# A hybrid transformer pair on one core: the latent's key and value products moved into the shared weight stream

## The reference, cut to what matters

```python
c_kv = rms_norm(c_kv, kv_norm_w)                       # 512 tokens x 128
k_rope = partial_rope(k_rope, cos, sin)
q_rope = partial_rope(q[..., :ROPE_DIM], ...)
# keys of 8 heads:   c_kv @ w_uk   (128 -> 8 x 48, padded with zeros to 8 x 64)
# values of 8 heads: c_kv @ w_uv   (128 -> 8 x 64)
# an indexer keeps the 128 best keys of each query; softmax over them; values
```

## Time and profile before

| what | value |
|---|---|
| median of 3 runs | 2507.4 us (2507.02 to 2508.23) |
| the profiled execution, its own time | 2504.52 us |
| its span, first to last instruction | 2502.8 us |
| TensorE matmul busy | 98% of the span |
| GpSimd, VectorE, ScalarE busy | 51%, 42%, 42% |
| chain that ended last | PE 90%, DVE 7%, ACT 3% |
| granted clock | 0.996 of full speed |
| DMA queue q1, share of 16 engines | 26.1% |

### The profile page before, as it was taken

One profiled execution on the slowest core, in us unless ns is written; L12 is line 12 of the kernel. 1 busy time (PEld: TensorE's weight loads), 2 busy tenths in 40 slices (PEclk: granted clock), 3 DMA queues, 4 the chain that ended last, 5 costly groups with the idle time before them and its releaser, 6 DMA issues.

```text
span 2502.8 us, 32082 instructions
## 1 busy us (share of the span) xinstructions
PE 2459.2 (98%) x12462; PEld 2014.1 (80%) x12462; DVE 1052.6 (42%) x2017; ACT 1042.2 (42%) x1584; POOL 1282.8 (51%) x1774
## 2 busy tenths in 40 slices
PE   8999999999999999999999999999999999999998
PEld 6777888888777787888878888877977788888886
DVE  7966525322795552422342113198265433311101
ACT  5334666323524467532443233332356524322221
POOL 5544645555553464555555554584433355554543
PEclk9999999999999999999999999999999999999999
DMA  4332112222222212232322232332222122232322
GB/s 156 93 104 75 60 59 82 89 100 96 92 92 72 85 51 76 68 99 95 111 93 100 93 101 85 135 110 69 92 69 68 65 96 98 89 100 94 100 94 83
DMA packets 63090, 224.45 MB, mean 90 GB/s; under 512 B 7335, under 2 KB 8871, under 8 KB 62812
## 3 DMA queue, kind: packets, MB, share of 16 engines
q1 hardware_dynamic: 61308, 216.62, 26.1%
q0 software_dynamic: 1632, 5.78, 0.8%
HBM read 219.70 MB, written 3.99 MB: 89 GB/s over the span
## 4 chain that ended last, share of the span: by engine, by line
PE 90%; DVE 7%; ACT 3%; issue 0%; DMA 0%; SPq 0%; DVEq 0%; ACTq 0%
PE proj L186 77%; PE proj L874 1%; PE att L911 1%; PE att L186 1%; DVE hT L543 1%; PE att L853 1%; PE att L897 1%; PE att L969 1%; PE att L864 1%; PE att L955 1%; DVE h_low L537 1%; PE att L2095 1%; ACT b_logits L2457 1%; ACT probs L1111 0%; PE att L2070 0%
## 5 line engine op out<-in xcount | busy, mean ns | idle before, releaser
L163 POOL TENSOR_TENSOR weight_low<-ring,weight_high 128x256 fp32r<-128x256 f32 x1584 | 1216.8, 800 | 1067.8 <-ACT weight_high L133 1046.1
L186 PE MATMUL proj<-h_high,weight_high 128*128 128x512 f32 x2000 | 787.4, 394 | 3.8 <-DVE h_low L537 1.5
L186 PE MATMUL proj<-h_high,weight_low 128*128 128x512 f32 x2000 | 779.4, 390 | 0.0
L186 PE MATMUL proj<-h_low,weight_high 128*128 128x512 f32 x2000 | 779.2, 390 | 0.0
L133 ACT ACTIVATE weight_high<-ring 128x1024 fp32r<-128x1024 f32 x391 | 412.0, 1054 | 406.9 <-PE proj L186 375.6
L186 PEld LDWEIGHTS proj<-h_high,weight_high 128*128 128x128 f32 x2000 | 375.6, 188 | 98.6 <-ACT sq_ L1010 5.3
L186 PEld LDWEIGHTS proj<-h_low,weight_high 128*128 128x128 f32 x2000 | 375.6, 188 | 79.0
L186 PEld LDWEIGHTS proj<-h_high,weight_low 128*128 128x128 f32 x2000 | 375.9, 188 | 75.2
L2678 DVE TENSOR_TENSOR b_big<-proj,b_big 128x512 f32<-128x512 f32 x42 | 29.0, 691 | 376.3 <-PE proj L186 376.3
L186 PE MATMUL proj<-b_act_high,weight_high 128*128 128x512 f32 x352 | 137.4, 390 | 0.0
L186 PE MATMUL proj<-b_act_high,weight_low 128*128 128x512 f32 x352 | 137.1, 389 | 0.0
(11 more groups left out here) (481 smaller groups left out, 3606.1 us busy)
## 6 DMA issues: line engine op xcount, KB each, us to landing
ring<-in_stream SPq DMA_DIRECT2D x396, 512.0 KB, 3.3
xT<-in_x SPq DMA_DIRECT2D x4, 512.0 KB, 6.3
idx<-gate_rows POOLq DMA_DIRECT2D x8, 256.0 KB, 4.3
out<-hT SPq DMA_DIRECT2D x4, 512.0 KB, 2.7
bias_rows<-bias_row SPq DMA_DIRECT2D x2, 512.0 KB
b_logits<-in_mem POOLq DMA_DIRECT2D x1, 1024.0 KB, 5.6
bias_rows<-bias_row SPq DMA_DIRECT2D x1, 768.0 KB
consts<-in_const SPq DMA_DIRECT2D x1, 704.0 KB, 10.2
```

Source lines behind the costliest of these rows:

```text
L163: self.s_low.on(pool.tensor_tensor(self.low[:, c % self.slots, cols], self.raw[:, c % self.slots, cols], self.high[:, c % HIGH, cols], ALU ...
L186: mm = pe.matmul(out, a, b, start=(k == 0 and i == 0), stop=(k == n - 1 and i == 2))
```

## The change

The 128 x 128 pieces of the key weights and the 128 x 512 value weights become tiles of the weight stream, in the order in which they are used. Together they are one chunk per layer. The eight products per layer go through `Weights.product`: the latent is split into `ckv_high` (ScalarE, after the move of za1) and `ckv_low` (VectorE, after top-k round 6), and each plain matmul becomes three rounded ones. The two direct loads per layer disappear. The value groups are reordered: vv0 and vv1 follow sbk0, vv2 and vv3 follow sbk1, nothing follows sbk2 and sbk3. As one key piece of 128 columns lies between dense tiles, chunks no longer end where groups end: chunk 17 of the layer ends inside sbq1 (step 6 of 0 to 7), 18 in sbq2 (step 5), 19 in sbq3 (step 4), 20 in sbk0 (step 3), and chunk 21 holds the rest of sbk0 and all value weights, so its last user is vv3. From sbk1 on a dense tile is a whole chunk again.

```diff
 def layer_tiles():
-    t += [(f"{n}{i}", KD, P) for n in ("q", "za", "zb", "sbq", "sbk") for i in range(4)]
+    t += [(f"{n}{i}", KD, P) for n in ("q", "za", "zb") for i in range(4)]
+    for i in range(4):
+        t += [(f"sbq{i}", KD, P), (f"kk{i}", 1, P)]
+    t += [("sbk0", KD, P), ("vv", 1, T)] + [(f"sbk{i}", KD, P) for i in range(1, 4)]
...
+LATENT_VALUES = [(0, 1), (2, 3), (), ()]
...
-                pe.wait_ge(s_ckv.sem, s_ckv.base + 1)
-                pe.wait_ge(s_lat.sem, s_lat.base + 32)
-            G.close(pe.matmul(out[:, :], wuk[:, i * P:(i + 1) * P], ckv, start=True, stop=True))
-        for b in range(TB):
-            dense(f"sbk{b}")
-            out = G.open(pe, f"vv{b}")
-            G.close(pe.matmul(out[:, :], ckv[:, b * P:(b + 1) * P], wuv, start=True, stop=True))
+                pe.wait_ge(s_ckv_low.sem, s_ckv_low.base + 1)
+            W.product(pe, f"kk{i}", out[:, :], [(ckv_high, ckv_low)])
+        for i in range(4):
+            dense(f"sbk{i}")
+            for b in LATENT_VALUES[i]:
+                out = G.open(pe, f"vv{b}")
+                c = slice(b * P, (b + 1) * P)
+                W.product(pe, f"vv{b}", out[:, :], [(ckv_high[:, c], ckv_low[:, c])], tokens=True)
...
             move(f"za{i}", za[:, i, :], ACT.Silu)
+            if i == 1:
+                act.wait_ge(s_ckv.sem, s_ckv.base + 1)
+                s_ckv_high.on(act.activation(ckv_high, ckv, ACT.Copy))
...
-        for b in range(TB):
-            if b == 0 and l == 0:
+        for i in range(4):
+            if i == 0 and l == 0:
                 act.wait_ge(S.s_rows.sem, 16)
-            move(f"sbk{b}", sk[:, b, :])
-            if b == 0:
+            move(f"sbk{i}", sk[:, i, :])
+            if i == 0:
                 act.wait_ge(s_rq.sem, s_rq.base + 4)
-            move(f"vv{b}", dv[:, b, :])
+            for b in LATENT_VALUES[i]:
+                move(f"vv{b}", dv[:, b, :])
...
+        def latent_low():
+
+            dve.wait_ge(s_ckv_high.sem, s_ckv_high.base + 1)
+            s_ckv_low.on(dve.tensor_tensor(ckv_low, ckv, ckv_high, ALU.subtract))
...
+            if i == 6:
+                latent_low()
...
-        s_lat.on(sp.dma_start(wuk, A["wuk"][l]), 16)
-        s_lat.on(sp.dma_start(wuv, A["wuv"][l]), 16)
```

More of the change, by code:

```diff
@@ L228, in layer_tile_of @@
             of[f"{n}{i}"] = f"{n}_half{i // TB}"
+    for b in range(TB):
+        of[f"vv{b}"] = "vv"
     return of
@@ L255, in layer_groups @@
     for i in range(4):
-        g += [(f"sbk{i}", "a"), (f"vv{i}", "a")]
+        g += [(f"sbk{i}", "a")] + [(f"vv{b}", "a") for b in LATENT_VALUES[i]]
     for p in range(PAIRS_H):
@@ L622, in hybrid_layers @@
     onehot, table, toep = flat_v[:, 0:ROW], flat_v[0:33, ROW:ROW + 12], flat_k[0:12, 0:ROW]
+    ckv_high, ckv_low = (rounded(n, [P, T], mix_at + 4 * (CAUSAL + i * T))[:, :] for n, i in (("ckv_high", 2), ("ckv_low", 3)))
     mlo, zc = sq_, sk
@@ L649, in hybrid_layers @@
     key_turn = tflat[KEY:KEY + 32, 3 * T:4 * T]
-    s_lat = sem("s_lat", 32)
+    s_ckv_high = sem("s_ckv_high", 1)
+    s_ckv_low = sem("s_ckv_low", 1)
     s_signs = sem("s_signs", 1)
@@ L1645, in keys @@
             s_keys.on(sp.dma_start(dk[64 * hh:64 * hh + ROPE, :, :], src), 16)
-    return {"keys": keys, "lead": lead_of(DEPTH), "both_vecs": both_vecs, "consts": consts, "onehot": onehot, "table": table, "loads": loads, "spread": spread,
+    return {"keys": keys, "lead": lead_of(DEPTH), "both_vecs": both_vecs, "consts": consts, "onehot": onehot, "table": table, "spread": spread,
             "first_scalar": first_scalar, "first_vector": first_vector, "tensor": tensor, "scalar": scalar, "vector": vector, "gpsimd": gpsimd}
@@ L3097, in lay_out_first @@
     C = columns()
-    A = {k: [] for k in ("vec", "wuk", "wuv")}
+    A = {k: [] for k in ("vec",)}
     stream = {}
@@ L3128, in lay_out_first @@
         uk[:, :, ROPE:] = I["w_dsa_uk"][l]
-        A["wuk"].append(uk.reshape(P, -1))
-        A["wuv"].append(I["w_dsa_uv"][l].reshape(P, -1))
+        uk = uk.reshape(P, -1)
+        stream.update({f"{l}.kk{i}": uk[:, i * P:(i + 1) * P] for i in range(4)})
+        stream[f"{l}.vv"] = I["w_dsa_uv"][l].reshape(P, -1)
     A = {k: np.ascontiguousarray(np.stack(v)) for k, v in A.items()}
@@ L3257, in both_blocks @@
         rotated = {S.W.place[f"{l}.sbk1"][0] // UNIT + RAW: l for l in range(DEPTH)}
-        latent = {S.W.place[f"{l}.idx0"][0] // UNIT + RAW + 1: l for l in range(DEPTH)}
         with nc.Block() as block:
@@ L3280, in _ @@
                         one["spread"](sp, c // 4 - 4)
-                    if c in latent:
-                        one["loads"](sp, latent[c])
                     if c in rotated:
```

2 lines of the change are left out of this document (removed).

## The result

The changed kernel takes 2508.91 us where the kernel before, on the same chip, takes 2505.34: ratio 1.0017, 95% interval 1.001 to 1.0024, thus +4.2 us with +2.5 and +6.0 as bounds. A ratio here is estimated over all executions of both kernels, so it need not be that of the two medians (these lie 3.6 us apart). Run again on two other chips it gave 1.0021 (1.0013 to 1.003) and 1.0031 (1.0019 to 1.0043). That is about the +4.6 us of the sum, and slower by no more than can just be told from nothing.

The account below looks back on a forecast made before the run. TensorE, busy 98% of the span, was taken as the bound, with resumes after products set by ScalarE's bank move. Layer terms of +2.2 and +2.4 made +4.6 us: 2512.0 us against the median 2507.4, range 2506.0 to 2516.5.

Parts of the forecast that it names:

- the sum: Both layers' terms added: +2.2 us in layer 0, +2.4 in layer 1, together +4.6 us.
- Keys, 0: Dense groups after each kk: three rounded matmuls for a plain product save 0, since the saving is inside the wait.
- E: The moment at which the dense group's last matmul is followed by the product on TensorE.
- The rival that the array's time was the limit: At 16 products, their own end sets the resume: -4.5 us, less 1.9 if the copy costs; 2502.9 to 2504.8; chance 0.10.
- The copy ahead of sbq1's move, +0.27: ScalarE copies chunk 20 first, so sbq1's move starts at E+0.47 instead of E+0.20: +0.27 us a layer.
- Values in pairs, -0.45: From the first value product to the scores, vv products in pairs take 3.44 us instead of 3.89: -0.45 a layer.
- The query turns, +1.41 and +1.66: Late fourth turn on VectorE delays vv0's move and sbk1: +1.3 and +1.55 us by layer, plus 0.11 each for a weight load.
- the walk: Placing GpSimd's chunks against VectorE's four turns: fourth turn ends near 145.4 in layer 0, 759.8 in layer 1.
- The rival with the turns fully under GpSimd: All turn operations slowed, vv0's move late, sbk1 behind it: +9.9 us or 2517.3 at its bound, 2514.7 at half; chance 0.25.
- The rival in which the turns stay in time: Query turns cause no wait; without the turn terms +1.5 us, 2508.9; chance 0.12.
- The chunk copy behind the exponentials, +0.95: Chunk 26's copy falls ahead of sbv0's move on ScalarE, making sbv2 wait longer: +0.95 us a layer, bounds 0 and 1.05.
- At nothing: Items priced at no cost: ckv_high, stream loads with DMA at 36%, GpSimd's extra 2.83 us, top-k's later end, chunk 24.

Follow-up runs that it names:

- the kernel with three edits: Changed kernel with chunk copy ahead of the exponentials, bias-row copies behind later chunks, and query turns one top-k round earlier: 1.0004 (0.9995 to 1.0012), 2506.57 us.
- the first trace: First profiled execution of the changed kernel, with no further edit: 2512.70 us, 3.8 us above its median.

## Why the prediction was right, point by point

**Keys, 0: right.** The resume is at E+0.85 before and after, and taking two of three matmuls away moved nothing. The rival that the array's time was the limit falls: the stretch didn't shorten. The Trainium skill (FP8 and Floating Point Precision, TensorE Precision Notes) prices true fp32 at four passes, so that three parts should save a quarter of each product; the rows agree where nothing waits for a bank: 0.95 us from the plain vv3 to the scores, and (49.19 - 8 x 5.44) / 8 = 0.71 for a rounded product inside a dense group. None of it shows where a product ends a group, because there the bank and not the array was waited for.

**The copy ahead of sbq1's move, +0.27: 0.33.** The wait is 0.76 for 0.43.

**Values in pairs, -0.45: -0.35.** The stretch of the kernel with three edits is 51.48; less the 0.33 it is 51.15, against 51.50. The step took sbk1's and sbk2's weight loads for hidden; in that kernel they still wait 0.21 and 0.15 for ScalarE's move of vv0 and vv2, so they are exposed.

**The query turns, +1.41 and +1.66: about +0.7 in each.** The mechanism is as told: sbk1 waits for dv, dv for the fourth turn, and two of the fourth turn's operations lie under a GpSimd chunk at 1.11 each. The size was off. The kernel with the bias rows later, against that with three edits, gives 52.16 - 51.48 = 0.68. The walk's terms were mis-sized, the first most of all: it put `latent_low` at 1.10 + gap under GpSimd in both layers. It takes 0.69 in layer 1, in the line above, and in layer 0

```profile
108.07 0.93 DVE L1341 TENSOR_TENSOR ckv_low<-idx,ckv_high 128x512 fp32r<-128x512 f32 x1
```

and in layer 1 the first turn starts only 0.61 later against sbq0 than before. The first two turns then lose less than before, as two operations of the first had been slowed already (1.20 and 1.11, now 1.26 and 0.69); the third and fourth lose 0.47 and 0.84. The fourth ends 1.48 later against sbq0 where the walk had 2.23, and E itself is 0.43 later and not 0.27: the fourth ends at E+1.63, not near E+2.5. A walk of four turns past a 2.8 us window on another engine adds up each placement error; the bounds of the wait, 0.1 and 4.1, held it, nearer the lower one. The rival with the turns fully under GpSimd falls: it wanted the fourth turn to end later than E+2.6. The rival in which the turns stay in time falls too, by the releaser of sbk1's load. Its 2508.9 us is the measured time to the digit, but from a time of before that was 2.1 too high; its +1.5 lies outside +2.5 to +6.0.

**The chunk copy behind the exponentials, +0.95: right**, in both layers, by the trace, by removing it, and by doing it alone.

**"At nothing": one of its items was not.** The loads: I costed the queue by the share of DMA, 36%, and not by the time of one load. A load that takes 8.27 us behind another transfer doesn't show in a mean share; the 6.7 us of the kernel before stood in its trace, and the copy is due earlier by the same splits that I priced at 0. In layer 0 it costs 0.1 to 1.1 us net where the clock holds, since it hides the wait for the turns, and 1.6 us more (clock 0.97 over the stretch of the first trace) where it falls. Chunks 24 and 25, the place where I did look for a late load, were in time.

**What the clock adds** stood in no step. At 8 of 14 places with the longer wait it fell, at 1.47 to 1.50 us each: estimated from these, 8/14 x 2 x 1.48 = 1.7 us for an average execution. Seven traces are few for such a share.

**The sum again.** Without the load a layer costs 0.33 - 0.35 + 0.68 + 0.95 = 1.61, both 3.2. The load adds 0.1 to 1.1 and the clock 1.7: 5.0 to 6.0, and more where the clock falls behind the load too. The three comparisons have 4.2 (2.5 to 6.0), 5.3 (3.3 to 7.5) and 7.8 (4.8 to 10.8). The predicted 4.6 was right partly by luck, because errors offset each other: the turns were over-sized by 1.7 us in all, and the clock (1.7) and the late load were missed. The absolute 2512.0 is 3.1 above 2508.91, of which 2.1 is the median of before, 2507.4 where more runs gave 2505.34.

**Open.** Why the load behind the bias rows takes 7.3 to 8.3 us: with those rows issued later it is gone in all four kernels, and with them there the six traces of the rewritten order all have it, but why 768 KB ahead cost 5 us more wasn't separated. And why the clock falls at one such place and holds at the next.

## What to carry to other kernels

When the release of a bank and not the arithmetic ends the wait, a cheaper product gains nothing: put the small product inside a long group, in the other bank, where neither its time nor the move is waited for. When a group is renamed or moved, list everything that hangs on its name in each engine's program, the copies that a `move` does on the way above all: one copy moved behind eight exponentials cost 0.95 us a layer, where the cheaper products gave 0.35 in that order. And cost a stream's load by its own issue and landing beside the other transfers in its queue, not by the share of DMA.

## What the runs showed of the hardware

**The clock after a wait of 2 us.** The granted clock, 1.00 before, was 0.5 to 0.6 for 3 to 4 us behind waits of 1.96 us at 8 of 14 places, and behind waits of 1.03 us at none of 10. I had taken a wait's price for its length; here a fall adds 1.5 us to it. The Trainium skill (TensorE: Matmul & The Clock Gate, Part 1) describes two levels, 1.2 and 2.4 GHz, set by how busy the array has been, and calls the number of matmuls at the lower one run-variable for one and the same kernel. The three traces of the changed kernel agree: a fall in one layer, in none, in both.

**A load behind another transfer.** 512 KB, issued 5.4 us behind the 768 KB of bias rows, landed after 8.27 us instead of 3.2 (7.3 to 8.3 in six traces); issued 6.0 us behind them, in the kernel before, after 6.7.

**VectorE beside GpSimd slows both.** 1.11 us for 0.69 on VectorE, and a chunk on GpSimd took 4.22 us beside the fourth turn, for 2.83 alone and 3.73 in the earlier trace rows.
